# A two-layer decoder trunk in float32 on one core: the beginnings of its four FFNs reordered, and the convolution mixer's helper work moved between engines

## The reference

```python
def reference(...):
    for l in range(DEPTH):
        x = x + 0.5 * swiglu(rms_norm(x, g_ffn1[l]), w_ffn1_gate[l], w_ffn1_up[l], w_ffn1_down[l])
        h = rms_norm(x, g_mix[l])
        if l % 2 == 0: x = x + conv_gating_mixer(h, ...)
        else:          x = x + stick_breaking_mixer(h, ...)
        x = x + 0.5 * swiglu(rms_norm(x, g_ffn2[l]), w_ffn2_gate[l], w_ffn2_up[l], w_ffn2_down[l])
    return rms_norm(x, g_final)

def conv_gating_mixer(h, ...):
    a_val, a_gate, u, v = jnp.split(h @ w_in, 4, axis=-1)          # 512 channels each
    a = a_val * sigmoid(a_gate)
    a = causal_depthwise_conv(a, conv_w, conv_b)                   # 31 taps
    a = silu(layer_norm(a, ln_a_g, ln_a_b))
    v = layer_norm(v.reshape(bsz, s, 4, 128), ln_v_g, ln_v_b)
    v = einsum("gts,bcsgd->bctgd", tril(sp_w), v) + sp_b           # chunks of 128 tokens
    return concatenate([a, u * v], axis=-1) @ w_out
```

## Time and profile before

| what | value |
|---|---|
| runs | 1955.20, 1963.94, 1970.75 us; median 1963.94 |
| profiled execution | 1964.64 us, its span on the core 1962.9 us |
| busy share of the span | PE 96%, PE weight loads 85%, DVE 71%, ACT 46%, POOL 28% |
| DMA | 247.27 MB, 126 GB/s mean |
| TensorE clock granted | 0.988 of full, mean |
| chain that ended last | PE 79%, DVE 10%, ACT 4%, DMA 3%, issue 2%, POOL 2% |

### The profile page before, as it was taken

How to read it: one execution, slowest core, us unless ns; L and a number is a source line. 1 busy time by engine, 2 the same in 40 slices (tenths; PEclk the granted TensorE clock), 3 DMA queues, 4 the chain that set the end, 5 groups by cost and what they waited for, 6 DMA issues and landing times.

```text
span 1962.9 us, 29292 instructions
## 1 busy us (share of the span) xinstructions
PE 1878.0 (96%) x11803; PEld 1677.6 (85%) x11803; DVE 1397.6 (71%) x1301; ACT 897.3 (46%) x1048; POOL 558.2 (28%) x399
## 2 busy tenths in 40 slices
PE   6899999999888999999999999999999988999998
PEld 6899988778667999987899998877888878999886
DVE  7777886589877787855687785654776677777753
...
GB/s 187 180 182 192 150 129 87 88 93 65 43 118 155 192 178 197 126 93 125 130 182 185 187 150 106 81 93 65 43 44 44 65 134 158 183 189 150 140 86 43
DMA packets 226362, 247.27 MB, mean 126 GB/s; under 512 B 7692, under 2 KB 194128, under 8 KB 225760
## 3 DMA queue, kind: packets, MB, share of 16 engines
...
## 4 chain that ended last, share of the span: by engine, by line
PE 79%; DVE 10%; ACT 4%; DMA 3%; issue 2%; POOL 2%; DVEq 0%; ACTq 0%; POOLq 0%
PE ps L395 26%; PE ps L397 25%; PE ps L396 25%; DMA stage<-in_w_ffn_gate_dram 3%; DVE y L1765 2%; DVE w_lo L1481 2%; PE ps L890 1%; PE ps L884 1%; DVE rinv L1471 1%; DVE w_lo L1452 1%; POOL chain L2079 1%; ACT w_hi L1041 1%; DVE x_sums L1644 0%; ACT w_hi L1005 0%; ACT hid L1262 0%
## 5 line engine op out<-in xcount | busy, mean ns | idle before, releaser
L395 PE MATMUL ps<-xs_hi,w_hi 128*128 128x256 f32 (+1 forms) x3168 | 977.0, 308 | 50.9 <-DVE w_lo L1481 38.1
L396 PE MATMUL ps<-xs_lo,w_hi 128*128 128x256 f32 (+1 forms) x3168 | 973.1, 307 | 0.0
L397 PE MATMUL ps<-xs_hi,w_lo 128*128 128x256 f32 (+1 forms) x3168 | 973.0, 307 | 0.0
L395 PEld LDWEIGHTS ps<-xs_hi,w_hi 128*128 128x128 f32 x3168 | 600.0, 189 | 93.4 <-DVE w_lo L1481 33.8
L397 PEld LDWEIGHTS ps<-xs_hi,w_lo 128*128 128x128 f32 x3168 | 599.9, 189 | 32.3
L396 PEld LDWEIGHTS ps<-xs_lo,w_hi 128*128 128x128 f32 x3168 | 600.1, 189 | 32.0
L1481 DVE TENSOR_TENSOR w_lo<-stage,w_hi 128x1024 fp32r<-128x1024 f32 x264 | 346.3, 1314 | 49.0 <-ACT w_hi L1041 49.0
L1481 DVE TENSOR_TENSOR w_lo<-chain,w_hi 128x1024 fp32r<-128x1024 f32 x132 | 161.4, 1222 | 116.9 <-ACT w_hi L1041 116.9
L1603 DVE TENSOR_TENSOR xs_lo<-hid,xs_hi 128x1024 fp32r<-128x1024 f32 x88 | 112.9, 1283 | 177.6 <-ACT xs_hi L1162 177.6
L1041 ACT ACTIVATE w_hi<-stage 128x1024 fp32r<-128x1024 f32 x176 | 180.7, 1050 | 87.4 <-PE ps L397 47.5
L2079 POOL TENSOR_TENSOR chain<-chain,stage 128x1024 f32<-128x1024 f32 x44 | 143.5, 3262 | 269.0 <-DVE w_lo L1481 269.0
...
## 6 DMA issues: line engine op xcount, KB each, us to landing
stage<-in_w_ffn_up_dram SPq DMA_DIRECT2D x88, 512.0 KB, 4.2
stage<-in_w_ffn_gate_dram SPq DMA_DIRECT2D x88, 512.0 KB, 5.9
stage<-in_w_ffn_down_dram SPq DMA_DIRECT2D x88, 512.0 KB, 3.8
stage<-in_w_ffn_gate_dram POOLq DMA_DIRECT2D x44, 512.0 KB, 9.1
chain<-in_w_ffn_up_dram SPq DMA_DIRECT2D x43, 512.0 KB, 7.4
chain<-in_w_ffn_gate_dram POOLq DMA_DIRECT2D x43, 512.0 KB, 7.6
stage<-in_w_qkv_dram SPq DMA_DIRECT2D x24, 512.0 KB, 4.6
stage<-in_w_in_ab_dram SPq DMA_DIRECT2D x16, 512.0 KB, 4.9
```

The costliest lines, as they stand in the source:

```text
L395: pe.matmul(to, a_hi, b_hi, start=start, stop=False, skip_group_check=True)
L396: pe.matmul(to, a_hi, b_lo, start=False, stop=False, skip_group_check=True)
L397: return pe.matmul(to, a_lo, b_hi, start=False, stop=stop, skip_group_check=True)
```

## The change

In the FFNs, GpSimd's list issues T3 of step 1 ahead of T4 of step 0 and of the fold; T2 of step 0 becomes an accumulating DMA from the weights in HBM (a second read of that gate block) in place of a GpSimd add. TensorE's `sum_folded` moves behind W21 of step 1. On VectorE and ScalarE the root, the reciprocal, `scale_gate` and the silu of step 0 move behind the splits up to T4 of step 1, and the silu of each step behind W21 of the next. For n = 0, ScalarE reads the upper four x tiles out of PSUM, and VectorE copies those four to `x_res` only behind the low part of W22.

In the mixer, the 62 diagonals are made by ScalarE, each a scaled copy of the identity; `lnv_g` and `lnv_b` are applied behind the spatial mix instead of ahead of it (which wants row sums of the spatial weights, one matmul, and `sp_shift`, four small VectorE instructions); the mix stands ahead of the late taps on TensorE; the low part of u * v moves to VectorE; the GpSimd sums become three more matmuls against ones for each of mean and variance; `TAPS_AT` deals 11 taps instead of 4 to the place ahead of v's means, and 19 instead of 18 are left for the end.

```diff
 gate_second, TensorE
-                gate_item(n, step, T1)
-                gate_item(n, step, W11)
+                for item in range(T2):
+                    gate_item(n, step, item)
+                pe.wait_ge(evicted, n * HF * EVICTS + 2)
                 sum_folded(n)
-                gate_item(n, step, T3)
+                for item in range(T2, ITEMS):
+                    gate_item(n, step, item)
                 pe.wait_ge(rms_made, NORM_FFN[n] + 1)
-                for item in range(W21, ITEMS):
-                    gate_item(n, step, item)
 gate_second, ScalarE
                 hi(n, Step(1), W21)
+                gate_mid(n, Step(1))
                 token_rms(NORM_FFN[n], stats_bank(n))
-                gate_mid(n, Step(1))
-                silu(n, Step(0))
                 copy_v(n, Step(1))
                 hi(n, Step(2), T1)
                 hi(n, Step(2), W11)
-                silu(n, Step(1))
+                silu(n, Step(0))
 add_first, GpSimd
                 add_t3(n, Step(0))
-                add_t2(n, Step(0))
+                pool.wait_ge(item_lo_made, n * FFN_ITEMS + T1 + 1)
+                pool.dma_start(Step(0).chain()..., gate_block(n, W22, Step(0)),
+                               accum_op=ALU.add).then_inc(t2_first_made, 16)
                 add_t1(n, Step(1))
+                add_t3(n, Step(1))
                 add_t4(n, Step(0))
                 fold_squares(n)
-                add_t3(n, Step(1))
 begin, VectorE
             x_rest(0)
+            lo(0, Step(0), W22)
+            for j in range(GROUP, DT):
+                x_copy(j)
 mixer, ScalarE
+            def diagonals(diag, part, k0, first, last):
+                for k in range(first, last):
+                    ins = act.activation(diag[:, k, :], ident[:, :], ACT.Copy, scale=part[:, k0 + k:k0 + k + 1].bitcast(F32))
+                return ins
 mixer, TensorE
+            pe.wait_ge(sp_ready, 1)
+            pe.matmul(ps[:, 2, :], ones[:, :], sp_rows[...], start=True, stop=True).then_inc(sp_summed, 1)
...
-            convolve_diagonal(7, diags_late, EARLY)
             for g in range(GB):
...
+            pe.wait_ge(diags_made, 4)
+            convolve_diagonal(3, diags_late, EARLY)
...
+                    elif n == 1 and m == 0:
+                        pe.wait_ge(b_made, GB)
+                        sum_rows(lambda i: y[:, i, :], ...).then_inc(y_mean_sum, 1)
                     elif n == 1 and m == 2:
                         pe.wait_ge(y_centred, CT)
+                        sum_rows(lambda i: v_cen[:, i]..., ...).then_inc(y_var_sum, 1)
-TAPS_AT = [10, 10, 8, 26, 4, 3, 6, 1, 3, 1]
+TAPS_AT = [10, 10, 8, 26, 11, 3, 2, 1]
```

More of the change, by code:

```diff
@@ L484, in load_ffn @@
                             sp.wait_ge(t4_made, n * HF + f)
[L485 to L486 removed]
+                        elif item == W22 and f > 1:
+                            sp.wait_ge(t2_made, n * (HF - 1) + f - 1)
                         load_block(n, item, Step(f))
@@ L775, in _ @@
             v_chunk(slot_of(c0 + 5), 4, 4, True).then_inc(w_used, 1)
+            pe.wait_ge(sp_ready, 1)
+            pe.matmul(ps[:, 2, :], ones[:, :], sp_rows[:, :, :].rearrange("p g t -> p (g t)"), start=True,
+                      stop=True).then_inc(sp_summed, 1)
             pe.wait_ge(a_val_scaled, CT)
@@ L794, in _, with sum_rows @@
                 mm.then_inc(mixed, 1)
+            pe.wait_ge(u_scaled, GB)
+            pe.wait_ge(diags_made, 4)
+            convolve_diagonal(3, diags_late, EARLY)
+            def sum_rows(tile_of, made):
+                for n, i in enumerate((PE_TILE, 0, 1, 2)):
+                    made(n)
+                    mm = pe.matmul(ps[:, 7, :], ones[:, :], tile_of(i), start=(n == 0), stop=(n == CT - 1))
+                return mm
             for n in range(4):
@@ L1030, in item_ready @@
                     act.wait_ge(t3_made, step.count(16, n * HF * 16 + 16))
+                elif item == T2 and step.first():
+                    act.wait_ge(t2_first_made, 16 * (n + 1))
                 elif item == T2:
-                    act.wait_ge(t2_made, step.count(1, n * HF + 1))
+                    act.wait_ge(t2_made, step.count(1, n * (HF - 1)))
                 elif item == T4:
@@ L1130, in gate_step @@
                 hi(n, step, W21)
+                silu(n, step.before())
                 gate_mid(n, step)
@@ L1134, in gate_step @@
                 hi(n, step.next(), W11)
-                silu(n, step)
             def row_used(n, e):
@@ L1169, in to_down @@
                 hi(n, end, W21)
+                silu(n, end.before())
                 gate_mid(n, end)
@@ L1538, in gate_first @@
                 step = Step(0)
-                lo(n, step, W22)
+                if n:
+                    lo(n, step, W22)
                 s57(n, step)
@@ L1559, in gate_second @@
                 lo(n, step, T4)
+                invert_rms(NORM_FFN[n])
+                scale_gate(n, Step(0))
+                lo(n, step.next(), T1)
+                lo(n, step.next(), W11)
                 make_hid(n, Step(0))
@@ L1562, in gate_second @@
                 c22(n, step)
-                lo(n, step.next(), T1)
                 c12(n, step)
                 scale_gate(n, step)
-                lo(n, step.next(), W11)
                 c21(n, step)
@@ L1571, in gate_step @@
                 lo(n, step, T3)
-                make_hid(n, Step(step.f - 1, step.i))
                 lo(n, step, W21)
+                make_hid(n, step.before())
                 lo(n, step, T2)
@@ L1610, in to_down @@
                 lo(n, end, T3)
-                make_hid(n, Step(HF - 2))
                 lo(n, end, W21)
+                make_hid(n, end.before())
                 lo(n, end, T2)
@@ L1824, in _ @@
             split_static(c0 + 7)
+            dve.wait_ge(sp_summed, 1)
+            dve.wait_ge(mixer_params, 16 * 2)
+            for g in range(GB):
+                ins = dve.scalar_tensor_tensor(sp_shift[:, g, :], ps[:, 2, g * P:(g + 1) * P],
+                                               params[:, ROW_LNV_B + g:ROW_LNV_B + g + 1], sp_bias[:, g, :], ALU.mult, ALU.add)
+            ins.then_inc(sp_shift_made, 1)
             dve.wait_ge(v_squared, TT)
@@ L1846, in _, with b_low @@
             scale_u(3)
+            dve.wait_ge(u_scaled, GB)
+            dve.wait_ge(sp_shift_made, 1)
+            def b_low(g):
+                dve.wait_ge(b_hi_made, g + 1)
+                dve.tensor_tensor(b_lo[:, g, :], u[:, g, :], b_hi[:, g, :].bitcast(F32), ALU.subtract).then_inc(b_lo_made, 1)
+            for g in range(GB):
+                dve.wait_ge(mixed, g + 1)
+                step(dve.scalar_tensor_tensor(v_cen[:, g].rearrange("p g c -> p (g c)").rearrange("p (t c) -> p t c", t=TT),
+                                              ps[:, 4 + g, :].rearrange("p (t c) -> p t c", t=TT),
+                                              params[:, ROW_LNV_G + g:ROW_LNV_G + g + 1],
+                                              sp_shift[:, g, :].unsqueeze(1).to_broadcast([P, TT, P]), ALU.mult, ALU.add))
+                dve.tensor_tensor(u[:, g, :], u[:, g, :], v_cen[:, g].rearrange("p g c -> p (g c)"),
+                                  ALU.mult).then_inc(b_made, 1)
+                if g:
+                    b_low(g - 1)
```

163 lines of the change are left out of this document (70 added, 93 removed).

## The result

| kernel | runs | median | ratio to before, 95% interval |
|---|---|---|---|
| before | 4 | 1964.6 us | |
| changed | 4 (1898.06 to 1905.93) | 1901.99 us | 0.9685 [0.9641, 0.9729] |

The account below looks back on a forecast made before the run. The prediction took PE, busy 96%, as the bound, with VectorE in layer 0's mixer: 1964.6 less 21.2 (FFNs), 12.5 (mixer) and 0.7 (median) gives 1930 us. Its own range was 1923 to 1936; the 8-in-10 range 1918 to 1949.

Parts of the forecast that it names:

- FFN 0, with the earlier start: Beginning of FFN 0: less idle and an earlier PE start, against a new stall of 2.4 ahead of T4; 0.6 us gained.
- FFN 1: Beginning of FFN 1: PE idle of 10.47 us becomes 3.3, with 1.3 of clock; 8.5 us gained.
- FFN 3: Beginning of FFN 3: PE idle of 11.67 us becomes 3.3, with 1.3 of clock; 9.7 us gained.
- T3 ahead of the fold: FFN beginnings: T3 of step 1, issued 7 us earlier or more, lands in time and its stall goes.
- T2 by DMA: FFNs 1 and 3: without GpSimd's add, the wait ahead of W21 falls from 2.31 us to about 0.1.
- Reciprocal behind T4: FFN beginnings: sum, reciprocal and scaling moved later leave one late stall, taken as 1.5 us in each FFN.
- The mixer: Mixer of layer 0, bound by VectorE: 8.5 us from an earlier last tap, 4.0 from the mean's wait; 12.5 (6 to 16).
- (a): FFN beginnings: VectorE piles up behind T4, two or three stalls of 1.5 instead of one; 1941 us, chance 0.18.
- (b): FFN beginnings: GpSimd's queue serves one DMA after the other, slower than before; 1989 us, chance 0.04.
- (c): Mixer: ScalarE's diagonals, at 0.63 each, hold up VectorE by delaying the sigmoid 6.3 us; 1936 us, chance 0.07.
- (d): FFNs and mixer: contention isn't GpSimd's, so slow x sums and slow taps stay; 1954 us, chance 0.05.
- (e): FFN beginnings: more gain than counted, none of the new stalls comes (9.7 us); 1920 us, chance 0.06.

Follow-up runs that it names:

- e7_after_off: The changed kernel with an unused tile of 32 bytes per partition behind params, which moves every tile behind it; 1926.44 us, ratio 0.9808 to before.
- e2_mixer: The kernel before with all mixer edits alone, the FFNs as before; 1933.90 us, ratio 0.9848.
- e5_gap: The kernel before with only an unused tile of 32 bytes per partition added behind params; 1946.47 us, ratio 0.9900.
- e6_xs_only: The kernel before with two unused tiles that move only xs_hi and xs_lo, to a multiple of 64 bytes; 1952.74 us, ratio 0.9935.
- e1_ffn: The kernel before with all FFN edits alone, the mixer as before; 1946.25 us, ratio 0.9902.

## Why the prediction was wrong

**The step that failed** is in the first paragraph: "only two things can shorten it: idle time of PE on the path, and matmuls saved", with 0.117 us per matmul taken as fixed. A third thing is the time of one matmul. With the unfavourable distance the changed kernel takes 1926.44 us, with the favourable one 1901.99. That is 24.5 of the 28.0 us missing, and the forecast of 1930 (1923 to 1936) was in effect one of e7_after_off. That e7_after_off comes so near to it is in part luck: its rest is 224 and not the 160 of before, its down projections are 0.5 us shorter each, and the changed kernel at 160 wasn't run.

Nor is the spacing worth one number, and the two things don't simply add. The 32 bytes alone gain 18.7 us on the kernel before, since its FFN code turns a part of the shorter matmul time into waits: pauses and slow clock in the gate phases, counted as above, are 68 to 70 us in e2_mixer, e5_gap and e6_xs_only for 63.1 before, but 43.6 in the changed kernel for 42.3 in e1_ffn. So the FFN edits are worth 18.4 us at the old distance and 31.9 at the new one (1933.90 − 1901.99, of which some 5 are a larger share of 113.3), and the whole change 44.5 (1946.47 − 1901.99) with the new distance on both sides, where 34.6 was forecast.

**The terms, measured at the distance of before** (e1_ffn against before, stage by stage; the mean spacing rose from 118.27 to 118.66 ns, which takes 2.9 us off the sum, and pauses and slow clock alone fell by 20.8):

| term | forecast | e1_ffn |
|---|---|---|
| FFN 0, with the earlier start | 0.6 | 0.8 |
| FFN 1 | 8.5 | 7.2 |
| FFN 2 | 2.4 | 2.5 |
| FFN 3 | 9.7 | 7.9 |
| sum | 21.2 | 18.4 |

*T3 ahead of the fold*: right. *T2 by DMA*: right for FFN 1, half right for FFN 3, where the pause ahead of W21 is 1.05 in e1_ffn and 1.23 in the changed kernel, and 0.1 was forecast: there PE starts 5.5 us ahead of the end of that split (1538.06 to 1543.57), in FFN 1 4.5 (549.81 to 554.30), which the forecast, made from FFN 1's rows, passed over. *Reciprocal behind T4*: right in kind, one stall per FFN ahead of T3 of step 2, but 1.88 in e1_ffn (2.1 in the changed kernel) and not 1.5. The timeline of VectorE in the changed kernel has the reason; it shows the splits of T1 and W11 of step 2 in FFN 1:

```profile
591.72 1.22 DVE L1520 TENSOR_TENSOR w_lo<-chain,w_hi 128x1024 fp32r<-128x1024 f32 x1
593.28 3.23 DVE L1520 TENSOR_TENSOR w_lo<-stage,w_hi 128x1024 fp32r<-128x1024 f32 x1 [0.34 <-ACT w_hi L1056]
```

and GpSimd's beside it:

```profile
593.03 2.39 POOL L2138 TENSOR_TENSOR chain<-chain,stage 128x1024 f32<-128x1024 f32 x1 [8.67 <-DVE w_lo L1520]
```

W11's split costs 3.23 instead of 1.22 beside the T2 add of step 1. I had charged GpSimd's adds to the x sums and not to the splits behind them. It isn't one split alone: of 396 such splits 17 take over 2 us before and 44 in the changed kernel (none of them away from a GpSimd add), for the new order puts W11's beside the T2 add; in the middle steps no pause of PE shows it. *FFN 0*: right, a stall of 2.24 for 2.4.

**The mixer** gained 14.8 us for 12.5. Timeline of VectorE in the changed kernel (taps, then the mean):

```profile
429.57 18.92 DVE L1814 SCALAR_TENSOR_TENSOR y<-a_pad,taps,y 128x512 f32<-128x512 f32 x26
...
494.62 12.67 DVE L1814 SCALAR_TENSOR_TENSOR y<-a_pad,taps,y 128x512 f32<-128x512 f32 x19
508.90 2.48 DVE L1929 SCALAR_TENSOR_TENSOR y<-ps,y 128x512 f32<-128x512 f32 x4 [1.61 <-PE ps L806]
```

and of ScalarE, the first diagonals:

```profile
402.26 4.78 ACT L1330 ACTIVATE diags_early_hi<-ident,taps_hi 128x128 fp32r<-128x128 f32 x16
```

Taps cost 0.67 to 0.78 each in every group, about as forecast, where nine took 13.31 and six 10.34 beside GpSimd. The last tap ends 11.2 us nearer to the mixer's first matmul (507.3 − 372.0 = 135.3, before 527.3 − 380.8 = 146.5), forecast 8.5; the mean's wait is 1.61 for 1.3, against 5.32. The 2.7 too few are the waits of VectorE that I added and that didn't come: neither for the row-sum matmul nor for the mix, and 1.29 for the late taps. At equal distance the mixer's edits are worth 12.6 us (1946.47 − 1933.90; the four executions of e5_gap lie 10 us apart).

**The rivals.** (a) is not seen: one stall per FFN behind T4 (2.14 to 2.16, ahead of T3 of step 2). (b) falls: GpSimd's T3 for step 1 went out at 561.33, and ScalarE took it at 572.22 with PE's matmul as what it had waited for, so it had landed in under 10.9 us. (c) falls: a diagonal is 0.30 (16 in 4.78). (d) falls for sums (0.41 to 0.42 each now) and taps; the one tap that still takes 1.77 stands beside GpSimd's subtraction for `sp_lo`. Its price had a slip: by the prediction's own terms FFN 3 would have gained 6.2 and not 5.3, so 1953 and not 1954. (e) is not what happened either: the new stalls came, and the time fell for another reason.
